# Ranking in single-tile pieces, square sums between the units, scan input units ahead of the first level

## What is computed

```python
def rms_norm(x, g):
    xf = x.astype(jnp.float32)
    y = xf * lax.rsqrt(jnp.mean(xf * xf, axis=-1, keepdims=True) + EPS)
    return (y * g.astype(jnp.float32)).astype(x.dtype)

def peer(h, w_q, subkeys, u, v):              # 256 tokens, 8 heads, 128 x 128 experts, 16 of them per head
    q = (xc @ w_q).reshape(C, PEER_HEADS, 2, PEER_HALF)
    s = jnp.einsum('chpd,hpnd->chpn', q, subkeys)
    sv, si = lax.top_k(s, PEER_TOPK)                                    # key ranking: 16 of 128, twice per head
    cand = sv[:, :, 0, :, None] + sv[:, :, 1, None, :]
    best, pos = lax.top_k(cand.reshape(C, PEER_HEADS, 256), PEER_TOPK)  # pair ranking: 16 of 256
    ids = jnp.take_along_axis(cand_id, pos, axis=-1)                    # rows of the experts
    g = jax.nn.softmax(best, axis=-1)                                   # gates
    ue, ve = jnp.take(u, ids, axis=0), jnp.take(v, ids, axis=0)         # 8 KB per token and expert
    a = jax.nn.gelu(jnp.einsum('cd,chkd->chk', xc, ue))
    return jnp.einsum('chk,chkd->cd', g * a, ve)

# first block:   x = x + g1x * (o @ w_out);  hx2 = modulate(rmsnorm(x, ..), ..);  x = x + g2x * peer(hx2, ..)
# second block:  recurrence with decay exp(cum_t - cum_s) over q, k = 1 - f, v = i;  x = x + merged @ w_mix_out
#                x = x + cross_attention(rms_norm(x, ..)) ;  x = x + experts(rms_norm(x, ..)) ;  rms_norm(x, ..)
```

## Time and profile before

| | us |
|---|---|
| median of 3 runs | 1829.32 (1827.41 to 1833.85) |
| the profiled execution | 1831.67 |
| its span in the trace | 1829.8 |
| busy: PE, DVE, ACT, POOL | 1511.3, 841.5, 519.4, 282.0 |
| bytes moved by DMA | 571.31 MB, 312 GB/s over the span |

### The profile page before, as it was taken

The page is one execution under the profiler, slowest core; times in us unless marked ns, Lnnn a source line. Parts: engine busy times, 40 slices in busy tenths (PEclk is TensorE's granted clock), DMA queues, the critical chain, the costliest instruction groups (busy, mean ns, idle before and its releaser), DMA issues.

```text
span 1829.8 us, 20250 instructions
## 1 busy us (share of the span) xinstructions
PE 1511.3 (83%) x7580; PEld 910.6 (50%) x7580; DVE 841.5 (46%) x1926; ACT 519.4 (28%) x1317; POOL 282.0 (15%) x277
## 2 busy tenths in 40 slices
PE   8899997657666667666666989999889999999997
PEld 5487686213323222222322889877754445444442
DVE  1777725776657574747445878422221101010111
ACT  2113603444343333334333237212121111111111
POOL 0000001344343334344331000000000000000000
PEclk9998988887988878789787999999989999999999
DMA  9672034999999999999994534452529999999993
GB/s 362 229 268 78 1 114 172 418 421 425 426 412 415 407 422 410 419 417 421 427 427 208 188 104 161 146 199 92 233 110 430 430 425 431 427 432 431 431 402 121
DMA packets 65453, 571.31 MB, mean 312 GB/s; under 512 B 7520, under 2 KB 7776, under 8 KB 8416
## 3 DMA queue, kind: packets, MB, share of 16 engines
q0 software_dynamic: 39312, 286.28, 37.8%
q1 hardware_dynamic: 25344, 281.13, 37.8%
q10 hardware_dynamic: 720, 2.89, 0.4%
HBM read 569.22 MB, written 1.05 MB: 312 GB/s over the span
## 4 chain that ended last, share of the span: by engine, by line
PE 62%; DMA 18%; DVE 9%; issue 5%; ACT 4%; POOL 2%; POOLq 0%; DVEq 0%; ACTq 0%
PE bank L1355 18%; DMA big<-in_peer_dram,big 17%; PE bank L1198 8%; PE bank L1072 6%; PE bank L899 4%; PE bank L1372 3%; PE bank L1347 3%; PE bank L1019 2%; PE bank L903 2%; PE bank L1002 2%; POOL big L494 2%; PE bank L1263 2%; PE bank L858 1%; ACT big L814 1%; PE bank L1224 1%
## 5 line engine op out<-in xcount | busy, mean ns | idle before, releaser
L1072 PE MATMUL bank<-big 128*64 128x512 f32 x1024 | 322.1, 765 | 221.3 <-ACT big L647 221.2
L494 POOL DMA_INDIRECT big<-in_peer_dram,big x256 | 272.6, 1065 | 570.8 <-PE bank L1072 349.7
L1072 PEld LDWEIGHTS bank<-big 128*64 128x64 f32 x1024 | 75.2, 163 | 417.6 <-ACT big L647 306.6
L1355 PE MATMUL bank<-big 128*64 128x512 f32 x768 | 168.0, 592 | 1.3 <-ACT big L814 1.3
L641 ACT ACTIVATE big<-big 128x1 f32<-128x1 f32 x256 | 51.9, 203 | 391.2 <-DVE big L1646 196.3
L1938 DVE TENSOR_TENSOR big<-big,bank 128x512 f32<-128x512 f32 x16 | 11.0, 688 | 297.8 <-PE bank L1355 297.8
L1355 PE MATMUL bank<-big,misc 128*64 128x512 f32 x512 | 113.4, 594 | 9.7 <-ACT big L814 9.2
L1646 DVE SCALAR_TENSOR_TENSOR misc<-big 128x1024 f32<-128x1024 f32 x64 | 78.6, 1228 | 91.2 <-DMA big<-in_peer_dram,big 91.2
L1646 DVE SCALAR_TENSOR_TENSOR big<-big 128x1024 f32<-128x1024 f32 x64 | 78.6, 1227 | 81.5 <-DMA big<-in_peer_dram,big 81.5
L1355 PEld LDWEIGHTS bank<-big 128*64 128x64 f32 x768 | 65.5, 137 | 100.1 <-issue 100.1
L1198 PE MATMUL bank<-H,ring 128*128 128x256 f32 x448 | 102.4, 392 | 9.6 <-DVE H L1706 6.7
(11 more groups left out here) (372 smaller groups left out, 2180.3 us busy)
## 6 DMA issues: line engine op xcount, KB each, us to landing
big<-in_moe_down_dram SPq DMA_DIRECT2D x32, 2048.0 KB, 11.2
big<-in_moe_up_dram SPq DMA_DIRECT2D x32, 2048.0 KB, 15.0
ring<-in_first_dram SPq DMA_DIRECT2D x37, 1024.0 KB, 7.6
ring<-in_second_dram SPq DMA_DIRECT2D x36, 1024.0 KB, 4.9
big<-in_moe_gate_dram SPq DMA_DIRECT2D x16, 2048.0 KB, 12.1
ring<-in_moe_gate_dram SPq DMA_DIRECT2D x16, 2048.0 KB, 12.2
misc<-in_mod_rest_dram POOLq DMA_DIRECT2D x16, 1024.0 KB, 5.4
big<-in_peer_dram,big POOLq DMA_INDIRECT x256, 10.1
```

What stands on the lines that cost most here:

```text
L494: pool.indirect_dma_start(out=gathered[b % GATHERS], out_offset=None, in_=t["peer"], in_offset=bass.IndirectOffsetOnAxis(ap=rows[:, b:b + ...
L1072: last = nc.tensor.matmul(bank[2 * tt + half][HALF * g:HALF * (g + 1), :], diag[:, b % DIAGS, :], gathered[b % GATHERS][:, a:a + 512], sta ...
L1355: last = nc.tensor.matmul(out[c, :], slots[:, c], weights[a], start=(k == 0), stop=(k == n - 1))
```

## The change

Three things are changed. (1) The ranking functions take one token tile or both. The keys of head h+2 are ranked for the first half at s = 26 and 29, the second half of the keys of head h+1 at 0 and 3, its pairs at 6 and 9, one tile in each; the expert rows move from 11 to 12, the gates on DVE from 14 to 15, ACT's exponential from 11 to 13. Head 0 ranks key 2 in full at s = 0. (2) In the three stages with a norm, the ones-product of unit n-1 is made after unit n; only the last stands behind all units. (3) The four units i are projected before the first level; the 16 parts are spread over all levels, and the taps evenly. ACT rounds the first two parts and takes the units i after the exponential of level 0.

```diff
--- before.py
+++ after.py
@@ -77,10 +77,10 @@
 SECOND_ACT = [u for u in SECOND if u[0] not in ("co", "ho", "mix", "xo")]
 
-PARTS_AT = (0, 0, 3, 3, 3, 3, 2, 2)
+PARTS_AT = (3, 2, 2, 2, 2, 2, 2, 1)
...
 TAPS_EARLY = (62, 10, 9, 4)
-TAPS_AT = (8, 8, 4, 3, 3, 3, 4, 6)
+TAPS_AT = (5, 5, 5, 5, 5, 5, 5, 4)
...
@@ -671,7 +671,7 @@
                     if s in (8, 13):
                         take_scores(2 * h + 4 + (8, 13).index(s))
                 if h + 1 < PH:
-                    if s == 11:
+                    if s == 13:
                         gate_exp(h + 1)
                     if s == 24:
                         take_gate(h + 1)
@@ -731,15 +731,15 @@
             act.wait_ge(S("f_ready"), 1)
             act.activation(DE, ff.rearrange("p c t -> p (c t)"), ACT.Ln).then_inc(S("logf_ready"), 1)
             take2([("q", i) for i in range(4)])
-            lead2(0)
-            lead2(1)
             for lev in range(LEVELS + 2):
 
                 if lev <= LEVELS:
                     act.wait_ge(S("dist_ready"), lev + 1)
                     act.activation(DE, DE, ACT.Exp).then_inc(S("decay_ready"), 1)
-                if lev in (1, 2):
-                    take2([("i", 2 * lev - 2), ("i", 2 * lev - 1)])
+                if lev == 0:
+                    lead2(0)
+                    take2([("i", i) for i in range(4)])
+                    lead2(1)
                 if lev >= 1:
                     for m in range(PARTS[lev - 1], PARTS[lev]):
                         take2(BETWEEN[m:m + 1])
@@ -991,6 +991,12 @@
 
             pe.wait_ge(S("o_taken"), 16)
             pe.wait_ge(S("od_normed"), 2)
+            def sum_x1(k):
+                pe.wait_ge(S("sq2_ready"), base("sq2_ready") + k + 1)
+                last = nc.tensor.matmul(bank[6][:, 0:T], ones, sq[:, k, 0:T], start=(k == 0), stop=(k == KT - 1))
+                if k == KT - 1:
+                    last.then_inc(S("ss2_ready"), 1)
+
             for n in range(8):
                 w = take()
                 b = bank[2 + n % 4]
@@ -1001,10 +1007,9 @@
                 for k in range(KT):
                     last = nc.tensor.matmul(b[:, 0:T], w[:, k, :], oT[:, k, :], start=(k == 0), stop=(k == KT - 1))
                 last.then_inc(S("first_unit_done"), 1)
-            for k in range(KT):
-                pe.wait_ge(S("sq2_ready"), base("sq2_ready") + k + 1)
-                last = nc.tensor.matmul(bank[6][:, 0:T], ones, sq[:, k, 0:T], start=(k == 0), stop=(k == KT - 1))
-            last.then_inc(S("ss2_ready"), 1)
+                if n >= 1:
+                    sum_x1(n - 1)
+            sum_x1(KT - 1)
 
             pe.wait_ge(S("subkeys_in"), 16)
             subkeys = three(work[:, 0:2048], 16)
@@ -1181,7 +1186,7 @@
                         last = nc.tensor.matmul(out, lo[:, k, :], h_hi[:, k, :], start=False, stop=(k == KT - 1))
                     last.then_inc(S("second_unit_done"), 1)
 
-            def project(units, rhs, ready=None):
+            def project(units, rhs, ready=None, after=None):
 
                 for what, i in units:
                     w, b = three(take2(what, i), KT), second_bank(what, i)
@@ -1197,10 +1202,18 @@
                                 pe.wait_ge(S(ready), base(ready) + k + 1)
                             last = nc.tensor.matmul(b[:, 0:T], w[:, k, :], rhs[:, k, :], start=(k == 0), stop=(k == KT - 1))
                     last.then_inc(S("second_unit_done"), 1)
+                    if after and i >= 1:
+                        after(i - 1)
+
+            def sum_square(squares, ready, done, k):
+                pe.wait_ge(S(ready), base(ready) + k + 1)
+                last = nc.tensor.matmul(bank[6][:, 0:T], ones, squares[:, k, 0:T], start=(k == 0), stop=(k == KT - 1))
+                if k == KT - 1:
+                    last.then_inc(S(done), 1)
 
             project([("ca", 0)], Hv, "H3_ready")
             project([("cg", 0)] + [(w, i) for i in range(1, 4) for w in ("ca", "cg")], Hv)
-            project([(w, i) for w in ("f", "q") for i in range(4)], Hv)
+            project([(w, i) for w in ("f", "q", "i") for i in range(4)], Hv)
 
             qe, ke = (x.rearrange("p (h t n) -> p h t n", h=4, t=TT) for x in (QE, KE))
             for lev in range(LEVELS + 2):
@@ -1223,9 +1236,7 @@
                                 (kk[:, h, tt * P:(tt + 1) * P], qq[:, h, tt * P:(tt + 1) * P])
                             last = nc.tensor.matmul(bank[4 + i // 4][:, (i % 4) * P:(i % 4 + 1) * P], a, b, start=True, stop=True)
                     last.then_inc(S("level_mm"), 1)
-                if lev < 2:
-                    project([("i", 2 * lev), ("i", 2 * lev + 1)], Hv)
-                if lev == 2:
+                if lev == 0:
                     pe.wait_ge(S("h3_lo_ready"), 1)
                 if lev <= LEVELS:
                     project_parts(range(PARTS[lev], PARTS[lev + 1]))
@@ -1264,11 +1275,8 @@
                                                     start=(k == 0), stop=(k == 3))
                     last.then_inc(S("second_unit_done"), 1)
             pe.wait_ge(S("merged"), 4)
-            project([("mix", i) for i in range(8)], gcs)
-            for k in range(KT):
-                pe.wait_ge(S("sqn_ready"), base("sqn_ready") + k + 1)
-                last = nc.tensor.matmul(bank[6][:, 0:T], ones, sqn[:, k, :], start=(k == 0), stop=(k == KT - 1))
-            last.then_inc(S("ssn_ready"), 1)
+            project([("mix", i) for i in range(8)], gcs, after=lambda k: sum_square(sqn, "sqn_ready", "ssn_ready", k))
+            sum_square(sqn, "sqn_ready", "ssn_ready", KT - 1)
 
             project([("xq", i) for i in range(8)], Hv, "H4_ready")
             pe.wait_ge(S("taken2"), len(SECOND_ACT))
@@ -1299,12 +1307,8 @@
                                                 xPT[:, h, kt, :], start=(kt == 0), stop=(kt == 1))
                 last.then_inc(S("xpv_ready"), 1)
             pe.wait_ge(S("xo_taken"), 4)
-            project([("xo", i) for i in range(8)], xo)
-
-            for k in range(KT):
-                pe.wait_ge(S("sq5_ready"), base("sq5_ready") + k + 1)
-                last = nc.tensor.matmul(bank[6][:, 0:T], ones, sq5[:, k, :], start=(k == 0), stop=(k == KT - 1))
-            last.then_inc(S("ss5_mm"), 1)
+            project([("xo", i) for i in range(8)], xo, after=lambda k: sum_square(sq5, "sq5_ready", "ss5_mm", k))
+            sum_square(sq5, "sq5_ready", "ss5_mm", KT - 1)
             pe.wait_ge(S("x4_ready"), base("x4_ready") + 8)
             pe.wait_ge(S("H5_ready"), base("H5_ready") + KT)
             pe.wait_ge(S("router_in"), 32)
@@ -1582,34 +1586,36 @@
 
             def top16(values, spare, out_v, out_i):
 
-                for tt in range(TT):
+                each_one = range(len(values))
+                for tt in each_one:
                     ins = dve.max(out_v[tt][:, 0:8], values[tt])
                 link(ins)
-                for tt in range(TT):
+                for tt in each_one:
                     dve.max_index(out_i[tt][:, 0:8], out_v[tt][:, 0:8], values[tt])
-                for tt in range(TT):
+                for tt in each_one:
                     ins = dve.match_replace(spare[tt], out_v[tt][:, 0:8], values[tt], -3.0e38)
                 link(ins)
-                for tt in range(TT):
+                for tt in each_one:
                     ins = dve.max(out_v[tt][:, 8:16], spare[tt])
                 link(ins)
-                for tt in range(TT):
+                for tt in each_one:
                     ins = dve.max_index(out_i[tt][:, 8:16], out_v[tt][:, 8:16], spare[tt])
                 return ins
 
-            def top_keys(n):
+            def top_keys(n, tts=range(TT)):
                 dve.wait_ge(S("sc_ready"), n + 1)
-                link(top16([sc[:, n % 4, tt, :] for tt in range(TT)], [sc2[:, tt, :] for tt in range(TT)],
-                           [sv[:, tt, n, :] for tt in range(TT)], [si[:, tt, n, :] for tt in range(TT)]))
-
-            def top_pairs(h):
-                for tt in range(TT):
+                link(top16([sc[:, n % 4, tt, :] for tt in tts], [sc2[:, tt, :] for tt in tts],
+                           [sv[:, tt, n, :] for tt in tts], [si[:, tt, n, :] for tt in tts]))
+
+            def top_pairs(h, tts=range(TT)):
+                for tt in tts:
                     ins = dve.tensor_tensor(three(cand[:, tt, :], PTOP), each(sv[:, tt, 2 * h, :], PTOP),
                                             wide(sv[:, tt, 2 * h + 1, :], PTOP), ALU.add)
                 link(ins)
-                link(top16([cand[:, tt, :] for tt in range(TT)], [cand2[:, tt, :] for tt in range(TT)],
-                           [best[:, h, tt, :] for tt in range(TT)], [pos[:, tt, :] for tt in range(TT)]))
-                dve.tensor_scalar(gmax[:, h, :].unsqueeze(2), best[:, h, :, 0:1], -1.0, None, ALU.mult).then_inc(S("best_ready"), 1)
+                link(top16([cand[:, tt, :] for tt in tts], [cand2[:, tt, :] for tt in tts],
```

(19 more changed lines are left out.)

## The result

The changed kernel took **1847.23 us** (median of 4 runs, 1843.2 to 1851.4), the kernel before 1831.59 us beside it: a ratio of 1.0082 [1.0062, 1.0103], 15.6 us more. The profiled execution of after took 1843.2 us, the shortest of its four, with a span of 1841.4 us. It is the span's stages that show where the time went.

What follows compares the result with a forecast made beforehand. DMA bounds the gather phase, where free buffers decide; PE's chain runs the projections and scan. Terms +18.6 + 3.3 - 5.6 = +16.3 us put the median at 1845.6 us (before: 1829.32), range 1817 to 1856.

Steps and rivals of the forecast that it cites:

- The supply of free buffers: Gather phase: buffer of block 12 free 14.5 us after landing, so block 19 lands at +21.5, not +17.0.
- The depth of the hole: Gather phase: block 19 lands 4.5 us late in each of seven ranking heads, +31.5 us in all.
- rival C: Gather phase: a ring load between blocks 12 and 19 relaxes the buffer limit, no hole opens; 1814.1 us; chance 0.17.
- that limit: Gather phase: a buffer must be free 10.0 us after its block landed, or DMA traffic has a hole.
- The lost DMA time: Gather phase: ranking in smaller pieces recovers all the DMA time lost below the full rate, -12.9 us.
- rival D: Gather and scan: pieces recover half the lost time, rest stays with expert rows; scan gains nothing; 1857.6 us; chance 0.09.
- The start: Start of the gather phase: key rankings delay the first dot, covered by seven gathers in flight; 0, bounds 0 to +1.1 us.
- part 1: Gather phase: ranking in pieces, with expert rows and exponential moved later, costs +18.6 us (+31.5 and -12.9).
- Part 2: Three norm stages: square sums between units expose add, square and table load; +3.3 us, bounds +1.5 and +4.
- Part 3: Scan: input units fill PE's wait before the first level, DVE then falls behind; -5.6 us, bounds -8.1 and 0.
- B: Gather phase: higher PE clock and quicker landing make the hole 2.1 us; whole -0.5, 1828.8 us; chance 0.19.

Runs made afterwards that it cites:

- exp12_sums_behind: The changed kernel with the gates' exponential at block 12 instead of 13 and the square sums put back behind their units: 1821.52 us, ratio 0.9949.
- exp_at_12: The changed kernel with the gates' exponential at block 12 instead of 13: 1828.77 us, ratio 0.9994 to the kernel before.
- exp10_sums_behind: The changed kernel with the gates' exponential at block 10 and the square sums put back behind their units: 1821.41 us, ratio 0.9947.
- rank_only: The kernel before with only the ranking in pieces and the moved expert rows, gates and exponential: 1848.58 us, ratio 1.0117.
- sums_only: The kernel before with only the square sums moved between the units, in all three stages: 1836.46 us, ratio 1.0036.
- warm_pe_short: The changed kernel with 14 unused products on TensorE ahead of the addition of blocks 12 and 13 in heads 0 to 6: 1837.38 us, ratio 1.0032.
- scan_only: The kernel before with only the scan's change (input units ahead of the first level, parts and taps spread): 1822.8 us, ratio 0.9963.
- no_tables: The changed kernel with a square replacing the gates' exponential in heads 1 to 7, so no table loads there: 1830.47 us, ratio 1.0001.

## Why the prediction was right, and where it wasn't

The forecast of 1845.6 us was 1.6 us below the measured 1847.2, and the sum of +16.3 us met +15.6. The sign and the mechanism hold. The terms are less good than their sum.

**The supply of free buffers** was read rightly from the dot of block 12 on. In the head shown this dot ends at 524.0; the table is back 4.6 us later (forecast 4.7), add_pair starts at 5.6 (5.7), POOL issues at 9.5 (9.6), and the gather issued then lands 7.64 us after that (7.0).

**The depth of the hole** was put at 4.5 us and is 3.3 in this head. The step that was mis-sized lies ahead of the dot: "the dot of block 11 ends at -1.2", that is, block 12 lands one pitch of 2.43 us after block 11. It lands later, because a load of the weight ring (1 MB) passes with the gathers at this place. The load's issue, and the DMA queues between 512 and 521 us of after (queue: packets, MB, share of 16 engines):

```profile
...
511.16 0.33 SPq L390 DMA_DIRECT2D ring<-in_first_dram  x1
```

```profile
...
q1 hardware_dynamic: 144, 1.05, 27.9%
```

It lands 8.9 us after its issue, at 520.06. From then on blocks come every 2.43 us again: counted back from block 14 (525.70, its dot has waited), block 12 lands at 520.8, 4.1 us after block 11. The expert rows have begun by then, and the dot of block 12 ends 3.2 us after the landing, not 4.9. The buffer is free at +12.7 instead of +14.5, block 19 lands at +20.4 instead of +21.5, and it was due at +17.0. So rival C's load takes 1.6 us off the hole, though it is over by block 12, as the forecast said.

The same load shows a slip in the forecast's reading of before. The pair (10, 11) was said to be freed "just at that limit" of 10.0 us. But the dot of block 10 starts at 503.19 and the pair is freed at 515.48, at least 12.3 us after the landing, and block 17 still comes on the pitch: there the load, issued at 501.38, passed between the landings of blocks 10 and 17 and made the limit 12.4 us.

Over the phase the holes of after are 19.1 us by the dots and 17.5 to 19.9 by the phase's length (after, less exp12_sums_behind or exp_at_12), 2.5 to 2.8 us a head, where the forecast had 31.5.

**The lost DMA time** of 12.9 us was the wrong step: "I let this recover all of the lost DMA time". The pieces recover less than half of it. exp_at_12, exp12_sums_behind and exp10_sums_behind put their net gain, the start included, at 2.6, 0.2 and 3.8 us; without the start's 2.9 us it is 3 to 7, each known to about 2 us. Windows of before in the head shown (columns as in the earlier trace rows) show what kind of time was lost:

```profile
...
515.00:525.00 10.00, 5.89 (x36) 2.13 (x36) 5.04 (x9) 3.38 (x12) 6.61 (x6) 0.84 0.96 367
525.00:535.00 10.00, 6.52 (x34) 2.12 (x30) 4.93 (x8) 3.38 (x12) 4.22 (x3) 0.67 1.02 426
520.00:535.00 15.00, 8.60 (x42) 2.71 (x38) 7.47 (x13) 5.07 (x18) 7.23 (x6) 0.76 1.00 400
```

The rate is 367 GB/s after the gather of block 17 was issued late (POOL waited 6.13 us; block 18 then lands 2.98 us after block 17), and 426 behind that. In later heads it falls further (605 to 610 us: 306 GB/s at a share of 0.89; 690 to 695: 315 at 0.88). So the low rates go with late buffers, and it was no mistake to count them as lost. But with the exponential in its cover the expert rows still make POOL wait 6.58 us (exp_at_12): the ranking in pieces does not bring these buffers early enough. That the rest stays with the expert rows is rival D's condition; no run took them away or split them, so this part is argued and not shown.

**The start** was put at 0, with 0 to +1.1 as bounds, and costs 2.9 us, known to 1.3 us (390 to 401 GB/s in the kernels without the pieces). "The seven gathers in flight cover about 15 us of this" holds for DMA's queue, but the eighth gather needs dot, ACT and PE for block 0 first, and these begin 7.6 us later. So part 1 is, in its own terms: hole +17.5 to +19.9, pieces -3 to -7, start +2.9, together +17.3 in after's phase (16.2 in rank_only's). Forecast: +31.5 - 12.9 + 0 = +18.6. Two terms were mis-sized, by 12 to 14 us and by 6 to 10 us, in opposite directions, and their errors cancelled. That the sum came within 1 us was luck; with only one of the two errors it would have been off by that much.

**Part 2** was +3.3 us by the covers that go. By the same events it is +0.9, +1.3, +1.3 in sums_only: the mechanism and the size hold. By the medians it is 7.1 us (4.6 to 8.8 by the interval). Missing in the forecast was TensorE's clock behind the stages: 1.2 us at the first block and 0.8 behind the mix square root; the remaining 1.5 us are not located. Had this term been in the sum, the two errors of part 1 would have cancelled less well.

**Part 3** was -5.6 and is -6.9 us. (Its two terms, -8.1 and +2.8, give -5.3; the 5.6 is the difference of the two starts named.) PE waits before levels 4, 5 and 6 (counted from 0), as forecast, and these come 0.46, 0.65 and 0.64 us late (8.00, 8.19 and 8.18 us apart against 7.54) instead of 0.7 each, since a level of DVE takes 8.18 us (8.25 forecast). Before level 7, where the forecast had another 0.7 us, PE does not wait. Together that is 1.05 us of the 1.3; the rest was not taken apart.

**Rivals.** B (hole half as deep, no change in time) is out as a whole: its higher clock was not granted (0.50 during the addition of 3.68 us); warm_pe_short shows what it is worth, 1.4 us a head, close to the 1.7 it was given. But its depth of 2.1 us a head was nearer to the measured 2.5 to 2.8 than the forecast's 4.5. By the Trainium skill, "DMA: Bandwidth & Descriptors", section "Anatomy of one DMA", the estimate for a gather of 1 MB was 4.4 us. The gather in the hole took 7.64 us from issue to landing, so the trace disagrees again. C needs a higher rate after the change; it fell, and its load came ahead of block 12's landing. D had half of the lost time recovered, about what happened, but with a scan that gains nothing, and scan_only gains 6.6 us.

The rule in "ScalarE: Activation LUTs", section "Rules for kernel authors", of the Trainium skill says to budget about 2.7 us for a change of table set. In after ACT's load stands at 525.33 and the exponential behind it starts at 526.63; the load back is at 527.34 and the gelu starts at 528.63. That is 1.3 us for each change. no_tables agrees: taking both away gave 2.1 us a head. The trace's duration is the right price here.

## What to carry to other kernels

Before counting lost bandwidth as gain, find the late buffers that lose it, and ask for each whether the change brings it earlier; cut the windows finely, since a mean of 400 GB/s at a share of 1.00 was 367 at 0.96 and 426 at 1.02. In a ring of buffers, write down the time from a block's landing to its free buffer against the limit, with every other load that passes on the same DMA engines in its place, and keep a second delay (here a table load on ACT) from falling behind the first (here VectorE's long step); under that step, or ahead of it, it cost nothing here. When a step is moved ahead of the first iteration of such a loop, count to the first reuse of a buffer, not to the end of the queue's initial filling.
